# VectorE's 32 by 32 transposes for the decay gates and the root, four row groups of 32 for the gates' products, and another order at the front

## The chip, the cores and the metric

The kernel runs on one core of a Trainium2 chip. The metric is the device time of one execution in microseconds (us). The numbers of the trace come from one profiled execution; its times count from the start of its span.

## What is computed

Two layers (DEPTH = 2) of a mixer on x of 512 tokens by 1024 channels, and a last RMS norm. In each layer (cut to what matters):

```python
h = rmsnorm(x, norm_g)
(qa, ka, va, ga, qb, kb, vb, ab, gb, cq, ckv, kr, gc, mg) = split_cols(h @ w_in)
# branch A: windowed attention; branch C: attention with a low-rank q and kv
# branch B, gated linear attention:
log_a = log_sigmoid(ab @ w_alpha + b_alpha) / B_GATE_TAU        # (512 x 16) @ (16 x 256)
yb = gla_chunk_readout(qb, kb, vb, log_a)
k_rope = apply_rope(kr, cos_c, sin_c)                           # 32 channels, one for all heads of C
m = sigmoid(mg)
y = m[:, :, 0] * za + m[:, :, 1] * zb + m[:, :, 2] * zc
return x + y @ w_out
```

## The kernel before

**Layout.** Channels lie on the partitions and the 512 tokens along the row, in most tensors. A few quantities are wanted the other way round ("natural": 128 tokens on the partitions, in TT = 4 tiles): the keys and values of B, the values of A, the 16 gate inputs ab and the 32 channels kr. They are columns of the four pieces PN1, whose products land in the four banks nat.

**Pieces.** All weights come as 154 pieces of 128 by 1024 (77 per layer), through three buffers raw. ScalarE rounds each piece to w_hi (split_hi, L909), VectorE takes the rest w_lo (split_lo, L1215), and TensorE makes three products for each tile, hi by hi, hi by lo and lo by hi (L657). A piece has four quarters of six products or so. Pieces 0 to 10 are PX (keys of A), PC[0], PC[1], the four PN1, PC[2], PQA[0], PQA[1] and PQB[0].

**Order.** make_schedule writes one list of steps by hand, SCHEDULE, and each engine walks through it in order and does its own part of every step. Nothing is reordered on an engine; between engines semaphores decide. VectorE makes the w_lo of piece p + 2 at quarter 1 of piece p, ScalarE the w_hi of piece p + 3 at quarter 3. Around the change the list is: pieces 0 and 1 with "sum_split" in between (the summed squares of x are split), piece 2, half of piece 3, "rms" (their mean by a product with ones, then logarithm and exponential on ScalarE, one Newton step on VectorE: rstd), "early" (the rope products of the key, two latents), piece 4, **rstd_nat**, lat_sum, piece 5, **rope_k**, piece 6, half of piece 7, **turn_ab**, the other half, **gla_gate**, piece 8, half of piece 9, gla_decay, k_dec.

**The steps that the change touches.**
- rstd_nat: TensorE transposes rstd (L775, four of 128x128) into the bank aux, and VectorE copies one column of each (L1351), so that the root of each token lies on its partition.
- At the end of piece 6 VectorE scales ab and kr by it into k_ab (128 tokens by 4 tiles by 48, L1567) and turns kr by its rope (L1572 to L1576); ScalarE scales A's values (L1006).
- turn_ab: TensorE transposes k_ab (L781, four) into aux, ScalarE copies rows 32 to 47 to ab1, whose row 48 is ones and carries the bias, and rows 0 to 31 to k_rot (L1046, L1048).
- gla_gate: TensorE multiplies ab1 with the weights of the gates, alpha_all, over all 128 rows, most of them zeros in alpha_all (L787, four products, each two instructions). It waits for ab1 and for A's values. The results go to the four banks nat, one each.
- "begin" of a layer: two squares of x are summed, then VectorE makes three small things (L1301 to L1305): the negated sinks, ab1 filled with ones, and zeros ahead of A's values.
- The front: six warm-up products (L744, twelve instructions), the transfers of the first weights (in parts, "heads") and of par_all on ScalarE's queue (L931, L933), then first_pieces (L712 to L722).

Of the kernel before, what the change touches and what calls it, by code (L numbers as in the profile page):

```python
# [19 lines left out]
ALU = mybir.AluOpType  # L20
# [6 lines left out]
TT = S // P  # L27
# [25 lines left out]
WARM = 6  # L53
# [227 lines left out]
AUX = [s for s in SCHEDULE if s[0] in ("rms", "rstd_nat", "gla_end", "latent", "turn_ab")]  # L281
# [23 lines left out]
def build_hybrid_trunk(nc, x_t, pieces, params, alpha, tables, consts, final_g, out, k_rope_dram):  # L305
    with ExitStack() as ctx:
# [76 lines left out]
        k_ab = gates[:, 5, 0:TT * 48].rearrange("p (t n) -> p t n", t=TT)  # L383
        k_prod = gates[:, 5, TT * 48:TT * 112].rearrange("p (i t n) -> p i t n", i=4, t=TT)
# [34 lines left out]
        head_hi, head_lo = sig("head_hi", 0), sig("head_lo", 0)  # L419
# [6 lines left out]
        k_ab_set, k_ab_prod, k_ab_rot, ab_turned = sig("k_ab_set", 4), sig("k_ab_prod", 4), sig("k_ab_rot", 2), sig("ab_turned", 1)  # L426
# [11 lines left out]
        rstd_set = sig("rstd_set", 1)  # L438
        ones_row = sig("ones_row", 1)
# [136 lines left out]
        def _(pe):  # L576
# [121 lines left out]
            def first_pieces():  # L698

                jobs = [(p, k) for p in range(2) for k in range(2)] + [(p, k) for k in range(2, KT) for p in range(2)]  # L700
                for p, k in jobs:
                    if k == 0:
                        pe.wait_ge(proj_free.sem, proj_free.at(0, p - 2))
                        pe.wait_ge(head_hi.sem, p + 1)
                    elif k == 2:
                        pe.wait_ge(head_hi.sem, p + 3)
# [42 lines left out]
            for layer in range(DEPTH):  # L749
                u = 0  # L750
                for name, i in SCHEDULE:
# [150 lines left out]
        def _(act):  # L902
# [49 lines left out]
            head_hi_part(0)  # L952
# [15 lines left out]
            for layer in range(DEPTH):  # L968
                u = 0
                for name, i in SCHEDULE:  # L970
                    if name == "begin":
                        for n in range(1, LATE + 1):
                            square(layer, n)
                    elif name == "split_x" and layer + 1 < DEPTH:
                        split_x(layer + 1, i)
                    elif name == "quarter" and i % 4 == 3:
# [25 lines left out]
                        if p == PN1[3]:  # L1002
                            act.wait_ge(aux_free.sem, aux_free.at(layer, AUX.index(("rstd_nat", 0)) + 1))
                            for t in range(TT):
                                act.wait_ge(k_ab_set.sem, k_ab_set.at(layer, t + 1))
                                nc.scalar.activation(v_a[:, t, :], nat[t][:, 256:384], ACT.Copy,  # L1006
                                                     scale=rstd_nat[:, t:t + 1]).then_inc(v_a_set.sem, 1)
# [21 lines left out]
                        if p == PQB[0]:  # L1029
# [6 lines left out]
                            act.wait_ge(aux_free.sem, aux_free.at(layer, AUX.index(("turn_ab", 0)) + 1))  # L1036
# [145 lines left out]
        def _(dve):  # L1182
# [65 lines left out]
            dve.wait_ge(head_hi.sem, 1)  # L1248
            head_lo_half(*HEADS[0]).then_inc(head_lo.sem, 1)
            for j in range(KT):  # L1250
                split_x(0, j)
                if j in (1, 2):
                    for n in ((1,) if j == 1 else (2, 3)):
                        dve.wait_ge(head_hi.sem, n + 1)
                        head_lo_half(*HEADS[n]).then_inc(head_lo.sem, 1)
                elif j in (3, 4):
                    dve.wait_ge(hi_split.sem, hi_split.at(0, j - 2))
                    head_lo_half(j - 3, slice(512, 1024)).then_inc(lo_split.sem, 1)
            split_lo(0, 2)
            for n in range(LATE + 1, KT + 1):  # L1260
                add_square(-1, n)
            def add_first_rows():
# [30 lines left out]
            for layer in range(DEPTH):  # L1293
                u = 0
                for name, i in SCHEDULE:
                    if name == "split_x" and layer + 1 < DEPTH:
                        split_x(layer + 1, i)
                    elif name == "begin":
                        for n in range(1, LATE + 1):
                            add_square(layer, n)  # L1300
                        nc.vector.tensor_scalar(neg_sink[:, :], par_all[:, layer, SINKS:SINKS + A_HEADS], -1.0, None,  # L1301
# [32 lines left out]
                    elif name == "rope_k":  # L1334

                        dve.wait_ge(proj_free.sem, proj_free.at(layer, by_dve(first_output(PX) + 1)))
                        for g in range(A_KV):
                            rows = slice(32 * g, 32 * g + 32)
                            nc.vector.tensor_tensor(k_a[64 * g:64 * g + 32, :], work[rows, 0, :], work[rows, 1, :],
                                                    ALU.subtract).then_inc(rope_out.sem, 1)  # L1340
                            nc.vector.tensor_tensor(k_a[64 * g + 32:64 * g + 64, :], work[rows, 2, :], work[rows, 3, :],
                                                    ALU.add).then_inc(rope_out.sem, 1)
# [6 lines left out]
                    elif name == "rstd_nat":  # L1349
                        dve.wait_ge(aux_ready.sem, aux_ready.at(layer, u + 1))  # L1350
                        nc.vector.tensor_copy(rstd_nat[:, :], aux[:, :].rearrange("p (t n) -> p t n", t=TT)[:, :, 0]  # L1351
                                              ).then_inc(aux_free.sem, 1)
# [179 lines left out]
                    elif name == "quarter" and i % 4 == 1:  # L1532
                        if (layer, i) != (0, 1) and i // 4 != PUKV:
                            split_lo(layer, i // 4 + 2)
                    elif name == "quarter" and i % 4 == 3:
# [27 lines left out]
                        elif p == PN1[3]:  # L1563
                            evacuated(layer, p)
                            dve.wait_ge(aux_free.sem, aux_free.at(layer, AUX.index(("rstd_nat", 0)) + 1))
# [3 lines left out]
                            dve.wait_ge(k_ab_set.sem, k_ab_set.at(layer, TT))  # L1569
# [202 lines left out]
```

## Time and profile before

| | before |
|---|---|
| median of 3 runs | 932.1 us (931.98 to 932.19) |
| the profiled execution's own time | 931.54 us |
| its span | 929.7 us |
| TensorE products busy | 922.0 us, 99% |
| TensorE weight loads busy | 755.8 us, 81% |
| VectorE busy | 601.2 us, 65% |
| ScalarE busy | 387.2 us, 42% |
| mean granted TensorE clock | 0.999 |

A busy share of a product counts from its start to its modelled end, and products overlap: the full-size ones last 0.39 us and start 0.23 apart. So what an edit on TensorE is worth is read from starts, not from durations. The same holds for VectorE, where a 128x512 instruction lasts 0.69 us and the next one may start 0.60 behind it.

### The profile page before, as it was taken

The numbers are of one execution on the slowest core, as the hardware profiler recorded it, in microseconds if no ns is written. First come the engines' busy times: TensorE is split into PE (matmuls) and PEld (weight loads), VectorE is DVE, ScalarE is ACT, GpSimd is POOL, SyncE is SP. The second block draws the span as 40 slices with busy tenths as digits, with TensorE's granted clock in tenths as the row PEclk, the third lists the DMA queues.
The fourth block names the chain that finished last, engine by engine and source line by source line (L and its number), as shares of the span: only waits on it lengthen the run. The fifth ranks groups of instructions, "written<-read, shape, count | busy, mean of one in ns | idle before, by whom it ended". The sixth has DMA issues, their size and how long they took to land.

```text
span 929.7 us, 13082 instructions
## 1 busy us (share of the span) xinstructions
PE 922.0 (99%) x5108; PEld 755.8 (81%) x5108; DVE 601.2 (65%) x982; ACT 387.2 (42%) x724; POOL 0.2 (0%) x4
## 2 busy tenths in 40 slices
PE   9999999999999999999999999999999999999997
PEld 7988888888888777888889888888888887778886
DVE  7856467448757877575457664674477568876834
ACT  7453344324543454432444333442264425562324
POOL 0000000000000000000000000000000000000000
PEclk9999999999999999999999999999999999999999
DMA  7324324322434255422232333253234433454542
GB/s 292 136 70 147 114 69 136 113 91 80 140 122 140 85 151 150 145 92 90 91 113 91 95 108 106 68 163 109 91 92 143 140 114 109 122 156 136 146 127 90
DMA packets 43789, 110.98 MB, mean 119 GB/s; under 512 B 8592, under 2 KB 11408, under 8 KB 43600
## 3 DMA queue, kind: packets, MB, share of 16 engines
q1 hardware_dynamic: 39664, 104.82, 35.8%
q10 hardware_dynamic: 4064, 5.33, 2.2%
q8 instruction: 40, 0.66, 0.3%
q14 instruction: 21, 0.17, 0.1%
HBM read 85.41 MB, written 2.23 MB: 94 GB/s over the span
## 4 chain that ended last, share of the span: by engine, by line
PE 86%; DVE 5%; ACT 3%; SPq 2%; issue 1%; DMA 1%; ACTq 1%; DVEq 0%
PE ring L657 65%; PE nat L657 9%; PE nat L868 3%; PE aux L892 2%; SPq L495 1%; DVE w_lo L1215 1%; ACT work L1117 1%; PE nat L672 1%; PE nat L671 1%; PE nat L673 1%; DVE work L1514 1%; DMA raw<-pieces 1%; ACT w_hi L909 1%; PE ring L672 1%; PE ring L671 1%
## 5 line engine op out<-in xcount | busy, mean ns | idle before, releaser
L657 PE MATMUL ring<-act_hi,w_hi 128*128 128x512 f32 x784 | 308.7, 394 | 0.0
L657 PE MATMUL ring<-act_lo,w_hi 128*128 128x512 f32 x784 | 305.5, 390 | 0.0
L657 PE MATMUL ring<-act_hi,w_lo 128*128 128x512 f32 x784 | 305.2, 389 | 0.0
L909 ACT ACTIVATE w_hi<-raw 128x1024 fp32r<-128x1024 f32 x152 | 161.7, 1064 | 340.5 <-PE ring L657 275.5
L1215 DVE TENSOR_TENSOR w_lo<-raw,w_hi 128x1024 fp32r<-128x1024 f32 x152 | 184.6, 1216 | 82.7 <-ACT w_hi L909 82.3
L657 PEld LDWEIGHTS ring<-act_hi,w_hi 128*128 128x128 f32 x784 | 147.1, 188 | 38.2 <-issue 8.4
L657 PEld LDWEIGHTS ring<-act_hi,w_lo 128*128 128x128 f32 x784 | 147.2, 188 | 31.1
L657 PEld LDWEIGHTS ring<-act_lo,w_hi 128*128 128x128 f32 x784 | 147.2, 188 | 29.7
L1545 DVE SCALAR_TENSOR_TENSOR gates<-ring,rstd 128x512 f32<-128x512 f32 x72 | 49.3, 685 | 77.0 <-PE ring L657 76.8
L657 PE MATMUL ring<-y_hi,w_hi 128*128 128x512 f32 x192 | 74.9, 390 | 0.0
L657 PE MATMUL ring<-y_hi,w_lo 128*128 128x512 f32 x192 | 74.7, 389 | 0.0
L657 PE MATMUL ring<-y_lo,w_hi 128*128 128x512 f32 x192 | 74.7, 389 | 0.0
L1055 ACT ACTIVATE gates<-gates 128x512 f32<-128x512 f32 x72 | 45.1, 626 | 18.9 <-DVE gates L1545 18.9
L657 PE MATMUL nat<-w_hi,act_hi 128*128 128x512 f32 (+1 forms) x128 | 48.1, 376 | 0.3 <-DVE w_lo L1215 0.3
L657 PE MATMUL nat<-w_lo,act_hi 128*128 128x512 f32 (+1 forms) x128 | 47.8, 374 | 0.0
L657 PE MATMUL nat<-w_hi,act_lo 128*128 128x512 f32 (+1 forms) x128 | 47.8, 374 | 0.0
L1129 ACT ACTIVATE work<-nat,neg_top 128x256 f32<-128x256 f32 (+3 forms) x48 | 24.7, 530 | 43.9 <-DVE neg_top L1472 43.9
L657 PEld LDWEIGHTS ring<-y_hi,w_hi 128*128 128x128 f32 x192 | 36.0, 188 | 8.1 <-issue 0.7
L657 PEld LDWEIGHTS ring<-y_hi,w_lo 128*128 128x128 f32 x192 | 36.0, 188 | 7.5
L657 PEld LDWEIGHTS ring<-y_lo,w_hi 128*128 128x128 f32 x192 | 36.1, 188 | 7.4
L1595 DVE SCALAR_TENSOR_TENSOR gates<-gates,ring 128x512 f32<-128x512 f32 x32 | 21.9, 685 | 9.0 <-PE ring L657 8.9
L657 PEld LDWEIGHTS nat<-w_hi,act_hi 128*128 128x128 f32 x128 | 24.1, 188 | 3.9 <-DVE w_lo L1215 0.8
(227 smaller groups left out, 995.6 us busy)
## 6 DMA issues: line engine op xcount, KB each, us to landing
raw<-pieces SPq DMA_DIRECT2D x152, 512.0 KB, 3.5
bank_g<-work SPq DMA_DIRECT2D x120, 64.0 KB, 2.0
lat<-work SPq DMA_DIRECT2D x72, 64.0 KB, 2.0
bank_g<-work ACTq DMA_DIRECT2D x40, 64.0 KB, 2.2
xt<-x_t SPq DMA_DIRECT2D x8, 256.0 KB, 4.9
bank_a<-work SPq DMA_DIRECT2D x32, 64.0 KB, 2.0
bank_g<-bank_a SPq DMA_DIRECT2D x16, 128.0 KB, 3.9
out<-gates SPq DMA_DIRECT2D x7, 256.0 KB, 2.1
```

What stands on the lines that cost most here:

```text
L495: engine.dma_start(dst[32 * j:32 * j + 32, S * i:S * i + S], work[32 * i:32 * i + 32, 3 + j, :]).then_inc(placed.sem, 16)
L657: mm = pe.matmul(dst, stationary, moving, start=start and i == 0, stop=stop and i == 2)
L671: pe.matmul(bank, act_hi[:, k, ts], w_hi[:, slot, cols], start=k == 0, stop=False)
L672: pe.matmul(bank, act_lo[:, k, ts], w_hi[:, slot, cols], start=False, stop=False)
L868: mm = pe.matmul(nat[a][:, col:col + n], q, k, start=part == 0, stop=part == 2)
L892: mm = pe.matmul(o_t[r * 64:r * 64 + 64, place, :].rearrange("p (i n) -> p i n", i=4), v_c[:, b, h * C_V:(h + 1) * C_V], turned_c[2 - i % ...
L909: nc.scalar.activation(w_hi[:, n % HL, :], raw[:, n % RAW, :], ACT.Copy).then_inc(hi_split.sem, 1)
L1055: nc.scalar.activation(gates[:, j if j >= 4 else 8 + j, :], gates[:, j, :], ACT.Tanh).then_inc(gate_tanh.sem, 1)
L1129: one = nc.scalar.activation(prob[a][:, keys], nat[a][:, keys], ACT.Exp, scale=C_SCALE, bias=neg_top[:, i % 2, 4 * n + a:4 * n + a + 1], a ...
L1215: nc.vector.tensor_tensor(w_lo[:, n % HL, :], raw[:, n % RAW, :], w_hi[:, n % HL, :].bitcast(F32), ALU.subtract).then_inc(lo_split.sem, 1)
L1545: nc.vector.scalar_tensor_tensor(gates[:, j, :], res, 0.5, rstd[:, :], ALU.mult, ALU.mult).then_inc(proj_free.sem, 1)
L1595: nc.vector.scalar_tensor_tensor(merged[:, j, :] if b == 0 else tile, tile, 1.0, z, ALU.add, ALU.mult).then_inc(proj_free.sem, 1)
```

## The change

Four parts:
1. rstd_nat has no product any more. VectorE transposes rstd by itself, in four instructions (one for each group of 32 partitions, 32 by 128), into y_pre, and copies one column of each tile.
2. turn_ab has no product and nothing on ScalarE. k_ab grows to 64 columns a tile, the last 16 filled with ones. VectorE transposes the half with ab in sixteen 32 by 32 blocks into ab1, tile t on the partitions 32t to 32t + 31, and the half with kr in four instructions into k_rot.
3. The gates' four products each use one row group of 32 rows, and alpha_all holds the weights four times.
4. The front: one warm-up product less, par_all sent ahead of the first weights, the first w_hi made by VectorE, the split of piece 3 moved ahead of the last two squares on both engines, and the three small VectorE steps moved from "begin" to rope_k.

```diff
-WARM = 6
+WARM = 5
-AUX = [s for s in SCHEDULE if s[0] in ("rms", "rstd_nat", "gla_end", "latent", "turn_ab")]
+AUX = [s for s in SCHEDULE if s[0] in ("rms", "gla_end", "latent")]
@@ TensorE
-                    elif name == "rstd_nat":
-                        aux_bank(layer, u)
-                        pe.wait_ge(rstd_set.sem, rstd_set.at(layer, 1))
-                        for t in range(TT):
-                            mm = pe.transpose(aux[:, t * P:(t + 1) * P], rstd[:, t * P:(t + 1) * P], ident)
-                    elif name == "turn_ab":
-
-                        aux_bank(layer, u)
-                        pe.wait_ge(k_ab_rot.sem, k_ab_rot.at(layer, 2))
-                        for t in range(TT):
-                            mm = pe.transpose(aux[0:48, t * P:(t + 1) * P], k_ab[:, t, :], ident)
                     elif name == "gla_gate":
 
-                        pe.wait_ge(ab_turned.sem, ab_turned.at(layer, 1))
+                        pe.wait_ge(ab_turned.sem, ab_turned.at(layer, 4 * TT))
                         pe.wait_ge(v_a_set.sem, v_a_set.at(layer, TT))
                         for t in range(TT):
-                            mm = pe.matmul(nat_gate[:, t, :], ab1[:, t * P:(t + 1) * P], alpha_all[:, layer, :],
-                                           start=True, stop=True)
+                            rows = slice(32 * t, 32 * t + 32)
+                            mm = pe.matmul(nat_gate[:, t, :], ab1[rows, 0:P], alpha_all[rows, layer, :], start=True, stop=True)
@@ ScalarE
             for n in range(2):
                 p, cols = HEADS[n]
-                act.dma_start(raw[:, p, cols], pieces[p, :, cols]).then_inc(head_loaded[n].sem, 16)
                 if n == 0:
                     act.dma_start(par_all[:, :, :], params).then_inc(par_loaded.sem, 16)
+                act.dma_start(raw[:, p, cols], pieces[p, :, cols]).then_inc(head_loaded[n].sem, 16)
-            head_hi_part(0)
                     if name == "begin":
+                        if layer == 0:
+                            split_hi(0, RAW)
                         for n in range(1, LATE + 1):
                             square(layer, n)
                         if p + HL < PIECES:
-                            split_hi(layer, p + HL)
+                            if (layer, p) != (0, 0):
+                                split_hi(layer, p + HL)
-                    elif name == "turn_ab":
-                        act.wait_ge(aux_ready.sem, aux_ready.at(layer, u + 1))
-                        act.wait_ge(ones_row.sem, ones_row.at(layer, 1))
-                        nc.scalar.activation(ab1[32:32 + B_RANK, :], aux[32:32 + B_RANK, :],
-                                             ACT.Copy).then_inc(ab_turned.sem, 1)
-                        nc.scalar.activation(k_rot, aux[0:C_ROPE, :], ACT.Copy).then_inc(aux_free.sem, 1)
@@ VectorE
-            dve.wait_ge(head_hi.sem, 1)
-            head_lo_half(*HEADS[0]).then_inc(head_lo.sem, 1)
+            p, cols = HEADS[0]
+            dve.wait_ge(head_loaded[0].sem, 16)
+            nc.vector.tensor_copy(w_hi[:, p, cols], raw[:, p, cols]).then_inc(first_hi.sem, 1)
+            dve.wait_ge(first_hi.sem, 1)
+            head_lo_half(p, cols).then_inc(head_lo.sem, 1)
                     elif name == "begin":
+                        if layer == 0:
+                            split_lo(0, RAW)
                         for n in range(1, LATE + 1):
                             add_square(layer, n)
+                    elif name == "rope_k":
+                        rope_k(layer)
                         nc.vector.tensor_scalar(neg_sink[:, :], par_all[:, layer, SINKS:SINKS + A_HEADS], -1.0, None,
                                                 ALU.mult).then_inc(sink_neg.sem, 1)
                         nc.vector.memset(ab1, 1.0).then_inc(ones_row.sem, 1)
                     elif name == "rstd_nat":
-                        dve.wait_ge(aux_ready.sem, aux_ready.at(layer, u + 1))
-                        nc.vector.tensor_copy(rstd_nat[:, :], aux[:, :].rearrange("p (t n) -> p t n", t=TT)[:, :, 0]
-                                              ).then_inc(aux_free.sem, 1)
+                        turn = y_pre[:, 0:P].rearrange("p (t r) -> p t r", t=TT)
+                        dve.wait_ge(rstd_set.sem, rstd_set.at(layer, 1))
+                        for n in range(4):
+                            rows = slice(32 * n, 32 * n + 32)
+                            nc.vector.transpose(turn[rows], rstd[rows, :].rearrange("p (t n c) -> p t n c", t=TT, n=4)[:, :, n, :]
+                                                ).then_inc(rstd_turned.sem, 1)
+                        dve.wait_ge(rstd_turned.sem, rstd_turned.at(layer, 4))
+                        nc.vector.tensor_copy(rstd_nat[:, :], turn[:, :, 0]).then_inc(rstd_nat_set.sem, 1)
+                    elif name == "turn_ab":
+                        dve.wait_ge(ones_row.sem, ones_row.at(layer, 1))
+                        dve.wait_ge(k_ab_set.sem, k_ab_set.at(layer, TT + 1))
+                        dve.wait_ge(k_ab_rot.sem, k_ab_rot.at(layer, 2))
+                        for t in range(TT):
+                            for n in range(4):
+                                nc.vector.transpose(ab1[32 * t:32 * t + 32, 32 * n:32 * n + 32],
+                                                    k_ab[32 * n:32 * n + 32, t, 32:64]).then_inc(ab_turned.sem, 1)
+                        for n in range(4):
+                            nc.vector.transpose(k_rot.rearrange("p (t n r) -> p t n r", t=TT, n=4)[:, :, n, :],
+                                                k_ab[32 * n:32 * n + 32, :, 0:32]).then_inc(k_turned.sem, 1)
@@ end of piece 6 on VectorE
+                            nc.vector.memset(k_ab[:, :, 48:64], 1.0).then_inc(k_ab_set.sem, 1)
                             for t in range(TT):
-                                nc.vector.tensor_scalar(k_ab[:, t, :], nat[t][:, 384:432], rstd_nat[:, t:t + 1], None,
+                                nc.vector.tensor_scalar(k_ab[:, t, 0:48], nat[t][:, 384:432], rstd_nat[:, t:t + 1], None,
```

## Rows read from the trace of the kernel before

**Rows 1.** The page: busy us of TensorE, share of the span, instructions.

```profile
PE 922.0 (99%) x5108; PEld 755.8 (81%) x5108; DVE 601.2 (65%) x982; ACT 387.2 (42%) x724; POOL 0.2 (0%) x4
```

**Rows 2.** TensorE's waits: line, waited for, us in total, times, longest.

```profile
PE aux L744 <- DVE merged L1232: 1.2, 1, 1.2
PE aux L735 <- DMA bank_g<-work: 0.4, 2, 0.2
PE nat L657 <- DVE w_lo L1215: 0.3, 1, 0.3
```

**Rows 3.** Timeline of TensorE at rstd_nat, layer 0: start, us, engine, line, count.

```profile
33.26 0.60 PE L775 MATMUL aux<-con,rstd 128*128 128x128 f32 x4
...
33.90 0.36 PE L657 MATMUL nat<-w_hi,act_lo 128*128 128x432 f32 x1
34.09 0.36 PE L657 MATMUL nat<-w_lo,act_hi 128*128 128x432 f32 x1
```

**Rows 4.** Timeline of TensorE at gla_gate, layer 1, with the weight load (PEld).

```profile
507.24 1.71 PEld L787 LDWEIGHTS nat<-alpha_all,merged 128*128 128x128 f32 x8
...
507.47 1.89 PE L787 MATMUL nat<-alpha_all,merged 128*128 128x256 f32 x8
...
509.43 0.40 PE L657 MATMUL ring<-act_lo,w_hi 128*128 128x512 f32 x1
```

**Rows 5.** Timeline of TensorE at branch C's scores, second half.

```profile
303.40 1.04 PE L868 MATMUL nat<-bank_g,bank_a 32*128 32x256 f32 x16
...
304.81 0.50 PE L657 MATMUL ring<-y_hi,w_hi 128*128 128x512 f32 x1
305.14 0.39 PE L657 MATMUL ring<-y_lo,w_hi 128*128 128x512 f32 x1
```

**Rows 6.** Timeline of VectorE, layer 1, from rstd_nat to the last latent.

```profile
495.10 0.15 DVE L1351 COPY rstd_nat<-aux 128x4 f32<-128x4 f32 x1
495.17 0.67 DVE L1333 TENSOR_TENSOR merged<-merged 128x512 f32<-128x512 f32 x1
...
499.03 0.68 DVE L1341 TENSOR_TENSOR bank_a<-work 32x512 f32<-32x512 f32 x1
499.75 1.22 DVE L1215 TENSOR_TENSOR w_lo<-raw,w_hi 128x1024 fp32r<-128x1024 f32 x1
501.70 0.79 DVE L1567 TENSOR_SCALAR gates<-nat,rstd_nat 128x48 f32<-128x48 f32 x4 [0.72 <-PE nat L657]
...
503.19 0.22 DVE L1574 TENSOR_TENSOR gates<-gates 128x64 f32<-128x64 f32 x1
...
503.46 1.22 DVE L1215 TENSOR_TENSOR w_lo<-raw,w_hi 128x1024 fp32r<-128x1024 f32 x1
507.67 0.69 DVE L1584 TENSOR_TENSOR gates<-ring,rstd 128x512 f32<-128x512 f32 x1 [2.99 <-PE ring L657]
```

**Rows 7.** Timeline of VectorE at "begin", layer 1.

```profile
471.17 0.17 DVE L1301 TENSOR_SCALAR neg_sink<-par_all 128x8 f32<-128x8 f32 x1
...
471.92 1.16 DVE L1215 TENSOR_TENSOR w_lo<-raw,w_hi 128x1024 fp32r<-128x1024 f32 x1
```

**Rows 8.** Timeline of VectorE at the last of four transposes of gla_norm.

```profile
143.89 0.67 DVE L1412 STREAM_TRANSPOSE work<-bank_a 128x512 f32<-128x512 f32 x1
144.48 1.18 DVE L1215 TENSOR_TENSOR w_lo<-raw,w_hi 128x1024 fp32r<-128x1024 f32 x1
```

**Rows 9.** Timeline of ScalarE at "rms", layer 0.

```profile
24.13 1.28 ACT L1061 ACT_TABLE_LOAD   x1
26.41 0.69 ACT L914 ACTIVATE merged<-aux,eps 128x512 f32<-128x512 f32 x1 [0.99 <-PE aux L770]
```

**Rows 10.** Timeline at gla_decay, layer 1: VectorE's log_a and TensorE's products.

```profile
513.62 1.22 DVE L1360 SCALAR_TENSOR_TENSOR gates<-nat,gates 128x1024 f32<-128x1024 f32 x1 [2.41 <-ACT gates L1070]
...
517.41 1.89 PE L794 MATMUL nat<-gates,con 128*128 128x256 f32 x8
```

**Rows 11.** One line's instructions, L744: ns min/median/max, first and last start, forms.

```profile
L744 PE MATMUL aux<-merged x12: 380/634/796, 1.2 to 5.9; 128*128 128x256 f32 x12
```

More of the change, by code:

```diff
@@ L382, in build_hybrid_trunk @@
         latent = gates[:, 2:5, :]
-        k_ab = gates[:, 5, 0:TT * 48].rearrange("p (t n) -> p t n", t=TT)
-        k_prod = gates[:, 5, TT * 48:TT * 112].rearrange("p (i t n) -> p i t n", i=4, t=TT)
+        k_ab = gates[:, 5, 0:TT * 64].rearrange("p (t n) -> p t n", t=TT)
+        k_prod = gates[:, 5, TT * 64:TT * 128].rearrange("p (i t n) -> p i t n", i=4, t=TT)
         k_cos, k_sin = [con[:, K_TABLE + 64 * i:K_TABLE + 64 * i + 64].rearrange("p (t n) -> p t n", t=TT) for i in range(2)]
@@ L418, in build_hybrid_trunk @@
         head_loaded = [sig(f"head_loaded{n}", 0) for n in range(4)]
-        head_hi, head_lo = sig("head_hi", 0), sig("head_lo", 0)
+        first_hi, head_hi, head_lo = sig("first_hi", 0), sig("head_hi", 0), sig("head_lo", 0)
         eps_set, ones_set = sig("eps_set", 0), sig("ones_set", 0)
@@ L425, in build_hybrid_trunk @@
         ring_act = sig("ring_act", by_act(first_output(PIECES)))
-        k_ab_set, k_ab_prod, k_ab_rot, ab_turned = sig("k_ab_set", 4), sig("k_ab_prod", 4), sig("k_ab_rot", 2), sig("ab_turned", 1)
+        k_ab_set, k_ab_prod, k_ab_rot, ab_turned = sig("k_ab_set", TT + 1), sig("k_ab_prod", 4), sig("k_ab_rot", 2), sig("ab_turned", 4 * TT)
         q_placed = sig("q_placed", 256)
@@ L438, in build_hybrid_trunk @@
         rstd_set = sig("rstd_set", 1)
+        rstd_turned, rstd_nat_set, k_turned = sig("rstd_turned", TT), sig("rstd_nat_set", 1), sig("k_turned", 4)
         ones_row = sig("ones_row", 1)
@@ L703, in first_pieces @@
                         pe.wait_ge(proj_free.sem, proj_free.at(0, p - 2))
-                        pe.wait_ge(head_hi.sem, p + 1)
+                        pe.wait_ge((first_hi, head_hi)[p].sem, 1)
                     elif k == 2:
-                        pe.wait_ge(head_hi.sem, p + 3)
+                        pe.wait_ge(head_hi.sem, p + 2)
                     elif k == KT // 2:
@@ L1002, in _ @@
                         if p == PN1[3]:
-                            act.wait_ge(aux_free.sem, aux_free.at(layer, AUX.index(("rstd_nat", 0)) + 1))
+                            act.wait_ge(rstd_nat_set.sem, rstd_nat_set.at(layer, 1))
                             for t in range(TT):
-                                act.wait_ge(k_ab_set.sem, k_ab_set.at(layer, t + 1))
+                                act.wait_ge(k_ab_set.sem, k_ab_set.at(layer, t + 2))
                                 nc.scalar.activation(v_a[:, t, :], nat[t][:, 256:384], ACT.Copy,
@@ L1034, in _ @@
                             act.dma_start(v_as[64:128, :, :], v_a[0:64, :, :]).then_inc(v_shifted.sem, 16)
-                            act.wait_ge(aux_free.sem, aux_free.at(layer, AUX.index(("turn_ab", 0)) + 1))
+                            act.wait_ge(k_turned.sem, k_turned.at(layer, 4))
                             act.dma_start(k_rope_dram, k_rot).then_inc(k_rope_saved.sem, 16)
@@ L1253, in _ @@
                     for n in ((1,) if j == 1 else (2, 3)):
-                        dve.wait_ge(head_hi.sem, n + 1)
+                        dve.wait_ge(head_hi.sem, n)
                         head_lo_half(*HEADS[n]).then_inc(head_lo.sem, 1)
@@ L1261, in _, with rope_k @@
                 add_square(-1, n)
+            def rope_k(layer):
+                dve.wait_ge(proj_free.sem, proj_free.at(layer, by_dve(first_output(PX) + 1)))
+                for g in range(A_KV):
+                    rows = slice(32 * g, 32 * g + 32)
+                    nc.vector.tensor_tensor(k_a[64 * g:64 * g + 32, :], work[rows, 0, :], work[rows, 1, :],
+                                            ALU.subtract).then_inc(rope_out.sem, 1)
+                    nc.vector.tensor_tensor(k_a[64 * g + 32:64 * g + 64, :], work[rows, 2, :], work[rows, 3, :],
+                                            ALU.add).then_inc(rope_out.sem, 1)
             def add_first_rows():
@@ L1333, in _ @@
                         nc.vector.tensor_tensor(sq_sum, sq[0], sq[1], ALU.add).then_inc(lat_acc.sem, 1)
[L1334 to L1342, printed above, removed]
                     elif name == "k_dec":
@@ L1532, in _ @@
                     elif name == "quarter" and i % 4 == 1:
-                        if (layer, i) != (0, 1) and i // 4 != PUKV:
+                        if (layer, i) not in ((0, 1), (0, 5)) and i // 4 != PUKV:
                             split_lo(layer, i // 4 + 2)
@@ L1564, in _ @@
                             evacuated(layer, p)
-                            dve.wait_ge(aux_free.sem, aux_free.at(layer, AUX.index(("rstd_nat", 0)) + 1))
+                            dve.wait_ge(rstd_nat_set.sem, rstd_nat_set.at(layer, 1))
+                            nc.vector.memset(k_ab[:, :, 48:64], 1.0).then_inc(k_ab_set.sem, 1)
                             for t in range(TT):
-                                nc.vector.tensor_scalar(k_ab[:, t, :], nat[t][:, 384:432], rstd_nat[:, t:t + 1], None,
+                                nc.vector.tensor_scalar(k_ab[:, t, 0:48], nat[t][:, 384:432], rstd_nat[:, t:t + 1], None,
                                                         ALU.mult).then_inc(k_ab_set.sem, 1)
-                            dve.wait_ge(k_ab_set.sem, k_ab_set.at(layer, TT))
+                            dve.wait_ge(k_ab_set.sem, k_ab_set.at(layer, TT + 1))
                             k1, k2 = k_ab[:, :, 0:16], k_ab[:, :, 16:32]
@@ L1751 @@
     rows = np.zeros((P, DEPTH, B_HEADS * B_DK), x.dtype)
-    rows[32:32 + B_RANK] = w_alpha.transpose(1, 0, 2)
-    rows[32 + B_RANK] = b_alpha
+    for t in range(TT):
+        rows[32 * t:32 * t + B_RANK] = w_alpha.transpose(1, 0, 2)
+        rows[32 * t + B_RANK] = b_alpha
     arrays = {
```

## The prediction

> **What bounds the kernel now.** I read the page first, then TensorE's waits, then its order of time around the three steps that the diff touches, and last VectorE's. TensorE is busy for 922.0 of 929.7 us, and all the waits that TensorE's view lists sum to 1.9 us, 1.2 of them before its first warm-up product [rows 1, 2]. So the kernel is a queue of products in a fixed order: each product taken out is worth its step on TensorE, as long as nothing that TensorE waits for becomes late by more than its slack. The question is therefore what the change does to VectorE just ahead of the decay gates' products (gla_gate, L787), where their input ab1 comes from.
>
> **What TensorE loses in work.** A step is the distance of two starts. The four transposes of rstd_nat start at 33.26, the second piece product behind them at 33.90, one more at 34.09 [rows 3]. Without them the products would start at 33.26 and 33.46, so they cost 33.90 - 33.46 = 0.44 us. The four of turn_ab are as long and stand in the same pattern, in both layers, so I take the same price. Both together: 0.88 us per layer.
> The gates' eight products start at 507.47, and the second product behind them at 509.43; their first weight load was at 507.24 [rows 4]. In four row groups the nearest rows are the scores of branch C, 32 rows by 256 columns, four neighbours in four groups and four banks, as the new gates would be: 24 instructions (the 16 of the row and 8 left out) between 303.40 and 304.81, 59 ns each, then 0.33 us to the second product behind [rows 5]. Eight of them are 0.47 us, and from the first load to the second product behind them 0.47 + 0.33 = 0.80 us, where it was 509.43 - 507.24 = 2.19. That is 1.39 us less if the input is there. If the groups did not overlap, this would be about 0.1.
>
> **What VectorE gets.** In layer 1 it runs without a pause from the root's refinement to the w_lo of piece 8, and it has just 0.72 us of idle time, at 501.70, before the work of the gates begins [rows 6]. Along this chain I add:
> (a) rstd_nat: one copy with a step of 0.07 (495.10 to 495.17) becomes four transposes of 32 by 128 and a copy.
> (b) The step rope_k takes in three small ones from "begin" (the negated sinks and two memsets): 471.17 to 471.92, 0.75 us [rows 7].
> (c) A memset of 64 elements, 0.10 (an estimate: a little over the 0.07 step of the copy of 4 elements).
> (d) turn_ab: sixteen transposes of 32 by 32, then four of 32 by 128.
> No row has such a small transpose. A transpose of 128x512 lasts 0.67 us and a step of 0.59 follows it [rows 8]; TENSOR_TENSOR of 64 columns lasts 0.22 and of 512 0.69, so 1.05 ns a column. From this a 32-column transpose lasts 0.67 - 480 x 1.05 ns = 0.17 us and a 128-column one 0.26. What matters is whether the next may start before the last has ended. In most rows it may: of the two 64-wide ones that start at 503.19 each lasts 0.22, yet the w_lo behind both starts 0.27 later. In the rope of k it may not: each instruction works on another group of 32 partitions than the last, there is no wait between them, and the one at 499.03 lasts 0.68 and the next starts 0.72 behind it (all four steps there are 0.71 or 0.72) [rows 6]. The new transposes change their group at every instruction, as those do. So I take the nearest row: duration plus 0.035, that is 0.20 for each of the sixteen and 0.30 for the wide ones; the ends are 0.10 (overlapped) and 0.24 (if filling the transposer adds as long again as 32 columns, 0.034).
> The Trainium skill, page "VectorE: DVE Perf Modes", section "Two Vector instructions with no wait between them", states this as a rule: an instruction whose input or output begins in another quadrant than before starts only when all earlier ones have finished. The rope rows agree. The same page's section "The three transpose paths" lists VectorE's transpose as quicker than TensorE's, which alone would speak for the overlapped price and the first rival's time.
>
> The chain in layer 1, in starts: (a) three held steps of 0.30 + 0.26 to the copy + 0.03 = 1.20, then 0.07, so lat_sum starts at 496.37 instead of 495.17: 1.20 later. With (b) the w_lo of piece 8 starts at 499.75 + 1.95 = 501.70. It takes a step of 1.13, so the gates' input is scaled from 502.83; before, this waited for TensorE until 501.70. The memset 0.10, the work up to the next w_lo 503.46 - 501.70 = 1.76, that w_lo (piece 9) 1.13: the sixteen transposes start at 505.82. Fifteen held steps of 0.20 and one duration of 0.17: ab1 is ready at 508.99, for TensorE at 509.02. TensorE would have been there at 507.24 - 0.88 = 506.36. It waits **2.7 us**, and its second product behind the gates starts at 509.02 + 0.80 = 509.82 instead of 509.43: 0.39 us lost, though 2.3 us of its work are gone.
> Layer 0 has the same distances (copy 36.70, w_lo 45.08, same steps). It has the front too. The parameters' transfer ahead of the first weights, the first w_hi on VectorE, and one warm-up product less (two of the 12 instructions of L744) may let the first real product start up to 0.4 us earlier. The split of piece 3, put ahead of two squares, removes the wait of 0.3 us for w_lo [rows 2]. But both end at the same gate wait: TensorE only gets there earlier, while VectorE's chain starts with the logarithm at 26.41. That had 0.99 us of slack behind the table load, 24.13 + 1.28 = 25.41 [rows 9]. The moved split (1.05 us on ScalarE) puts the summed squares and so the table load 1.05 us later, to 26.46, and the logarithm at about 26.48, 0.07 late. So the front brings nothing, or costs 0.1.
> Moved VectorE work (b) frees "begin", where only that same sum waited for it. The four wide transposes for k behind ab1 last 4 x 0.30 = 1.2 us; behind them queue the latent's scaling (507.67 before, now about 510.3), ScalarE's three latent steps, and the gates' soft plus, all back to back. So log_a ends about 2.3 us later than at 514.84, at 517.2, and TensorE's decay products come at 517.41 + 0.39 = 517.8 (load about 0.2 before) [rows 6, 10]. They are just covered, with 0.4 us; the w_lo of pieces 6 to 11 have over 1 us each except that of piece 6, which lies ahead of (a) and does not move.
> **Sum:** 2 x 0.39 + 0.07 = +0.85 us. The profiled execution took 931.54 us (span 929.7) against a median of 932.1, so I put the difference on the median: **933.0 us**, 0.1% more, within the 0.2% (1.9 us) that a measurement can tell from no change.
>
> **Rivals.**
> 1. The small transposes overlap, as the 64-wide rows do: 0.10 and 0.20 a step. Then (a) costs 0.89, the sixteen 15 x 0.10 + 0.17 = 1.67, ab1 is ready at 507.21 and the second product behind starts at 508.01: 1.4 us won per layer, 2.8 in all, 929.3. The diff asks for no wait between them, which speaks for it; the rope rows speak against it. Chance 0.20.
> 2. Slower: each small transpose pays the filling of its 32 columns apart, 0.034 us more for each of twenty per layer. That is 0.68 per layer, 934.4. It decides from 0.024 us more per transpose (0.95 us over 40). For it: no row shows a transpose so short. Against it: the 128x512 one lasts no longer than a TENSOR_TENSOR. Chance 0.20.
> 3. TensorE's clock falls in the wait. It stands still for 2.7 us in layer 1 and about 3.4 in layer 0, where nothing before stood over 0.4. At the start the products of L744 last 0.63 us and only the last ones 0.38, after about 4 us of work [rows 11]; 4 us at half the clock is 2 us of work lost: 935.0 if in one layer, 937 in both. The page "TensorE: Matmul & The Clock Gate" of the Trainium skill, section "Why this matters for your kernels", asks for no idle gaps of this order between bursts. Chance 0.07.
> 4. The change does not do what it says: the gates' products don't run side by side. Then each layer loses 1.27 more, 935.5. The scores' rows speak against it. Chance 0.03.
> The forecast itself has 0.50, with an own range of 932.0 to 933.9 (0.02 us per transpose either way).
>
> **Numbers.** Faster by over 0.2% is below 930.2: rival 1 and a little for waits that I count too long, 0.21. Slower is above 934.0: rivals 2 to 4, 0.30. Within: 0.49. The range takes in rivals 1 and 2 and one fallen clock: 929.2 to 935.1.
>
> **What would show it.** In the new trace: a wait of TensorE at the gates' products for VectorE's transposes, 2.7 us in layer 1 and about 3.4 in layer 0; starts of the sixteen 0.20 apart; the gates' eight products within 0.5 us; no wait at the decay products; the wait of 0.3 us on w_lo gone. The prediction is wrong if those starts are 0.10 apart, or if TensorE waits elsewhere (the decay products first, whose slack is 0.4), or if ab1 is ready before 507.6 in layer 1's times of before, from where the change wins over 0.2%.

## The result and the profile after

| | before | after |
|---|---|---|
| median | 932.05 us (4 runs) | 937.26 us (4 runs, 937.06 to 938.64) |
| ratio, after to before | | 1.0062, 95% interval 1.0049 to 1.0074 |
| the profiled execution | 931.54 us | 937.12 us |
| its span | 929.7 us | 935.3 us |
| mean granted TensorE clock | 0.999 | 0.995 |

The change made the kernel 0.6% slower, 5.2 us. The forecast was 933.0 with a range of 929.2 to 935.1: the sign of the difference was right, its size was wrong, and the time lies outside the range. In the page, TensorE is busy for 1.0 us less than in [rows 1], though the span is 5.6 us longer:

```profile
span 935.3 us, 13088 instructions
...
PE 921.0 (98%) x5090; PEld 753.5 (81%) x5090; DVE 612.4 (65%) x1033; ACT 384.7 (41%) x719; POOL 0.2 (0%) x4
```

TensorE's waits (waited for: us in total, times, longest) answer to [rows 2]. The wait at piece 3 is gone, and a new one at the gates' products holds 6.5 us in two times:

```profile
PE nat L778 <- DVE merged L1358: 6.5, 2, 3.6
PE aux L745 <- DVE merged L1218: 1.2, 1, 1.2
PE aux L736 <- DMA bank_g<-work: 0.4, 2, 0.2
```

VectorE's order of time in layer 1, from rstd_nat to the last latent, answers to [rows 6]. It is one chain without a pause, as forecast:

```profile
497.97 1.30 DVE L1348 STREAM_TRANSPOSE y_pre<-rstd 32x128 f32<-32x128 f32 x4
499.31 0.17 DVE L1351 COPY rstd_nat<-y_pre 128x4 f32<-128x4 f32 x1
499.38 0.69 DVE L1336 TENSOR_TENSOR merged<-merged 128x512 f32<-128x512 f32 x1
...
503.97 0.17 DVE L1304 TENSOR_SCALAR neg_sink<-par_all 128x8 f32<-128x8 f32 x1
...
504.73 1.15 DVE L1201 TENSOR_TENSOR w_lo<-raw,w_hi 128x1024 fp32r<-128x1024 f32 x1
505.84 0.11 DVE L1576 MEMSET gates<- 128x64 f32 x1
505.88 0.71 DVE L1578 TENSOR_SCALAR gates<-nat,rstd_nat 128x48 f32<-128x48 f32 x4
...
507.58 1.22 DVE L1201 TENSOR_TENSOR w_lo<-raw,w_hi 128x1024 fp32r<-128x1024 f32 x1
508.71 3.71 DVE L1358 STREAM_TRANSPOSE merged<-gates 32x32 f32<-32x32 f32 x16
512.45 1.30 DVE L1361 STREAM_TRANSPOSE merged<-gates 32x128 f32<-32x128 f32 x4
```

And TensorE's order of time there, which answers to [rows 4]. After a standstill of 2.90 us come the gates' products, a first full-size product at the usual distance behind such a group (0.34; it is 0.33 in gate_later below), a second one that is followed after 0.39 instead of 0.23, and then products that last 0.63 us and start 0.43 apart:

```profile
509.19 0.39 PE L658 MATMUL ring<-act_hi,w_lo 128*128 128x512 f32 x1
512.48 0.71 PE L778 MATMUL nat<-alpha_all,merged 32*128 32x256 f32 x8 [2.90 <-DVE merged L1358]
513.12 0.50 PE L658 MATMUL ring<-act_hi,w_hi 128*128 128x512 f32 x1
513.46 0.59 PE L658 MATMUL ring<-act_lo,w_hi 128*128 128x512 f32 x1
513.85 0.63 PE L658 MATMUL ring<-act_hi,w_lo 128*128 128x512 f32 x1
514.27 0.63 PE L658 MATMUL ring<-act_hi,w_hi 128*128 128x512 f32 x1
...
516.83 0.43 PE L658 MATMUL ring<-act_hi,w_hi 128*128 128x512 f32 x1
```

That is the clock at its lower level, 1.2 GHz. In a table by stretches (from and to, length, busy time and count of PE, of PEld, of DVE, of ACT and of POOL, granted clock, DMA share, GB/s) it stands at 0.50 behind both gate waits; this is layer 1:

```profile
512.00:513.00 1.00, 0.52 (x8) 0.31 (x8) 0.91 (x4) 0.00 (x0) 0.00 (x0) 1.00 0.00 0
513.00:514.00 1.00, 1.00 (x7) 0.74 (x4) 0.91 (x4) 0.00 (x0) 0.00 (x0) 0.74 0.00 0
514.00:515.00 1.00, 1.00 (x4) 0.81 (x3) 0.47 (x1) 0.50 (x1) 0.00 (x0) 0.50 0.00 0
515.00:516.00 1.00, 1.00 (x4) 0.71 (x4) 0.69 (x1) 0.97 (x3) 0.00 (x0) 0.50 0.00 0
516.00:517.00 1.00, 1.00 (x4) 0.81 (x3) 0.65 (x1) 1.00 (x2) 0.00 (x0) 0.55 0.00 0
517.00:518.00 1.00, 1.00 (x6) 0.81 (x5) 0.04 (x1) 0.97 (x2) 0.00 (x0) 1.00 0.00 0
```

**Where the 5.6 us of the span come from.** The second product behind the gates is the mark that the prediction used. In layer 0 it starts at 52.28 instead of 51.05, so 1.23 us are lost there. Layer 1's rstd_nat comes at 497.97 instead of 495.10, 2.87 late, so 2.87 - 1.23 = 1.64 us were lost between, and the disturbance that stands in that stretch is the clock. (Product by product: when TensorE's steps are 0.23 again, at 56.38, it is 2.79 late, so 1.56 of the 1.64 lie in the slow products themselves, and 0.08 elsewhere.) In layer 1 the mark comes at 513.46 instead of 509.43, 4.03 late, so 1.16 lost at the gates. The span ends 5.60 late, 1.57 more. Together: 2.39 us at the gates, 3.21 us by the clock. This is the pair of profiled executions; the medians differ by 5.2 us.

### The profile page after: what moved, and what is told of

It reads as the page before. It is cut to its first block, busy times and chain, and to the rows that moved or that the text cites. A ratio compares the mean times of both kernels' runs of the same rounds, so it can differ in the third digit from the quotient of the medians.

```text
span 935.3 us, 13088 instructions
## 1 busy us (share of the span) xinstructions
PE 921.0 (98%) x5090; PEld 753.5 (81%) x5090; DVE 612.4 (65%) x1033; ACT 384.7 (41%) x719; POOL 0.2 (0%) x4
## 4 chain that ended last, share of the span: by engine, by line
PE 82%; DVE 9%; ACT 4%; issue 2%; SPq 1%; DMA 1%; ACTq 1%; DVEq 0%
PE ring L658 64%; PE nat L658 5%; PE nat L858 3%; PE aux L882 2%; DVE w_lo L1201 2%; SPq L496 1%; ACT work L1103 1%; ACT w_hi L899 1%; PE nat L674 1%; PE nat L672 1%; PE nat L673 1%; DVE work L1524 1%; DVE merged L1358 1%; PE ring L674 1%; PE ring L672 1%
## 5 line engine op out<-in xcount | busy, mean ns | idle before, releaser
L1524 DVE STREAM_TRANSPOSE work<-work 128x512 f32<-128x512 f32 x42 | 26.9, 683 | 0.0
```

Source lines behind the costliest of these rows:

```text
L1524: nc.vector.transpose(blocks[:, :, k, :, :].rearrange("p j h r -> p h j r"), prob[k].rearrange("p (h j c) -> p h j c", h=GROUP, j=4)).then ...
```

## The experiments

Two questions: what the transposes' price is made of, and whether the clock's fall follows from the standstill. Then, whether the chain ahead of the gates is all that spoils the change. The last experiments answer this by shortening the chain. The kernel before ran beside all of them, with a median of 931.8 us.

**fill_wait: products in the wait.**

```diff
                     elif name == "gla_gate":
+                        pe.wait_ge(aux_free.sem, aux_free.at(layer, 1))
+                        for _ in range(10):
+                            pe.matmul(aux[:, :], act_hi[:, 0, 0:P], act_hi[:, 0, :], start=True, stop=True)
                         pe.wait_ge(ab_turned.sem, ab_turned.at(layer, 4 * TT))
```

> The changed kernel with ten full-size products more on TensorE (0.23 us each, into the bank aux, results unused) in front of the wait for the gates' input, so that TensorE stands still for about 1.3 us in layer 0 and 0.6 us in layer 1, not 3.6 and 2.9. Theory: the fallen clock costs 1.6 us per layer, and it falls because of the standstill. Then the products behind the gates stay 0.23 us apart and the time is 937.3 - 3.2 = 934.1 us. Rival: the clock falls for another reason (the 32-row products themselves), then it stays at 937.3.

Measured: 934.01 us (933.69 to 934.88). TensorE's first wait in its list:

```profile
PE nat L781 <- DVE merged L1361: 1.9, 2, 1.3
```

The granted clock is 1.00 in every stretch around both gates, and the products behind the gates start at 52.14 and 52.47, and from there on 0.23 apart. The kernel does more work and is 3.25 us faster. So the fallen clock costs the 3.2 us that the two traces had shown, and it falls because TensorE stands still. The rival is excluded: the 32-row products were there as before.

**same_group: all small transposes on the same 32 partitions.**

```diff
-                                nc.vector.transpose(ab1[32 * t:32 * t + 32, 32 * n:32 * n + 32],
-                                                    k_ab[32 * n:32 * n + 32, t, 32:64])
+                                nc.vector.transpose(ab1[0:32, P * t + 32 * n:P * t + 32 * n + 32],
+                                                    k_ab[0:32, t, 32:64])
```

> The changed kernel with all sixteen small transposes reading and writing partitions 0 to 31 (their blocks beside each other along the row), so the gates' input is wrong and the output is not the reference's. Theory: a transpose that begins in another group of 32 partitions than the last waits for its end; inside one group the starts come closer, to 0.10 to 0.14 us from 0.23. The input is ready 1.5 to 2.0 us earlier per layer, and the clock may stay up: 931 to 934 us. Rival: filling the transposer sets the distance, whatever the group: 0.23 us as before and 937.3 us.

This kernel leaves out the spreading of the blocks over the groups, so its output is not the reference's; only its times are used. Measured: 929.86 us (929.64 to 931.69), ratio 0.9982 (0.9973 to 0.9992). VectorE at turn_ab in layer 0, and the line's durations (ns, least, median and most):

```profile
47.76 1.59 DVE L1358 STREAM_TRANSPOSE merged<-gates 32x32 f32<-32x32 f32 x16
...
L1358 DVE STREAM_TRANSPOSE merged<-gates x32: 156/156/193, 47.8 to 506.6; 32x32 f32<-32x32 f32 x32
```

Inside one group the sixteen take 1.59 us, so they start (1.59 - 0.16) / 15 = 0.095 apart and last 0.156. In the changed kernel they take 3.71:

```profile
L1358 DVE STREAM_TRANSPOSE merged<-gates x32: 193/202/207, 47.5 to 512.2; 32x32 f32<-32x32 f32 x32
```

They start (3.71 - 0.20) / 15 = 0.234 apart there and last 0.202. The held start is shown; the change of the group costs 0.14 us per transpose, 2.1 us per layer. The edit moves input and output to one group at once, so it doesn't tell which of the two matters. TensorE's waits shrank to 1.48 and 0.77 us, and the clock stayed at 1.00. It came out 1.1 us below the lower end of what I expected. The two prices add up to it: 2.1 us in each layer and the 3.2 us of the clock make 7.4, and 937.26 - 7.4 = 929.9.

**ab_first: turn_ab ahead of the w_lo of piece 9.**

```diff
     piece(PN1[3])
-    half(PC[2], 0)
     step(("turn_ab", 0))
+    half(PC[2], 0)
     half(PC[2], 1)
```

> The changed kernel with turn_ab ahead of the w_lo of piece 9 on VectorE. The input is ready 1.13 us earlier, so TensorE waits about 2.5 us in layer 0 and 1.8 in layer 1. If the clock stays up at that, 937.3 - 2.3 - 3.2 = 931.8 us; if it still falls in both layers, 935.0 us; in one, 933.4.

Measured: 934.39 us (934.13 to 935.42). The profiled execution is the slowest of the six, 935.42 us, and shows the outcome with the clock fallen in both layers. The input came 0.91 us earlier per layer, not 1.13: behind the last rope step, on whose result they wait, the transposes start after 0.35 us (506.64 and 506.99 in layer 1), where in the change the w_lo starts after 0.14. That gives 937.26 - 2 x 0.91 = 935.4, as this execution took. The other five took 934.1 to 934.6, about 1.0 less; whether the clock fell less in them can't be told without a trace of one. The standstills were 2.65 and 1.98 us, and behind both the clock is at 0.50 (the second shown; columns: stretch, length, busy share and count of PE, granted clock, DMA share, GB/s):

```profile
511.00:512.00 1.00, 1.00 (x11) 1.00 0.00 0
512.00:513.00 1.00, 1.00 (x5) 0.71 0.00 0
513.00:514.00 1.00, 1.00 (x4) 0.50 0.00 0
```

**split_back: piece 3 split where it was before** (the lines of the diff with split_hi(0, RAW) and split_lo(0, RAW) undone).

> The changed kernel with the split of piece 3 where it was before. Theory: in layer 0 TensorE only waits 0.5 us less at the gates, since the chain of VectorE sets their time and starts 0.1 us earlier: 937.1 to 937.3 us, unless the clock then stays up in layer 0 (a standstill of about 3.1 us; at 2.0 and 2.7 it fell). Rival: the split is worth its 0.5 us also here, 937.8.

Measured: 936.85 us (936.72 to 937.87), ratio 1.0057 (1.0043 to 1.0071) beside the change's 1.0062 (1.0049 to 1.0074), so by the times no difference that can be told. TensorE's waits at the gates are 5.8 us in all instead of 6.5, 2.88 in each layer, and the clock fell in both.

The trace shows more. The wait at piece 3 is gone here too: with the three small steps out of "begin", the w_lo of piece 3 starts at 21.64 instead of 22.08 before, and TensorE loses only about 0.2 us at piece 3. And the moved split is not free for VectorE's chain. ScalarE's logarithm, where that chain starts, comes 0.46 us earlier without it (this run, then the change):

```profile
26.04 0.69 ACT L904 ACTIVATE merged<-aux,eps 128x512 f32<-128x512 f32 x1 [0.59 <-PE aux L771]
26.50 0.69 ACT L904 ACTIVATE merged<-aux,eps 128x512 f32<-128x512 f32 x1
```

So in layer 0 the gates' input is ready 0.46 us earlier too: their products start at 50.84 instead of 51.30. The split's gain is absorbed by the gate wait, and its price of 0.46 us is paid there. The medians lie 0.4 us apart in that sense, which agrees but is too little to prove it.

In layer 0 of this execution the clock was down before work had begun again, and the gates' eight products already ran slowly: 1.16 us to the next one, not 0.64 (TensorE, then the stretches with the columns of ab_first's):

```profile
50.84 1.23 PE L778 MATMUL nat<-alpha_all,merged 32*128 32x256 f32 x8 [2.88 <-DVE merged L1353]
52.00 0.80 PE L658 MATMUL ring<-act_hi,w_hi 128*128 128x512 f32 x1
52.60 0.63 PE L658 MATMUL ring<-act_lo,w_hi 128*128 128x512 f32 x1
```

```profile
50.00:51.00 1.00, 0.16 (x4) 0.57 0.06 25
51.00:52.00 1.00, 1.00 (x8) 0.50 0.06 16
```

This fall cost 2.8 us: from the gates' start at 50.84 the fourteenth full-size product is reached at 57.38, 6.54 us later, where the steps at the upper level (0.98 to the second product, then twelve of 0.23) would make 3.74. The one in layer 1, behind a standstill of the same 2.88 us, cost 1.6. So the price of a fall is not the same each time. The profiled execution took 937.87 us, 1.0 over the median, which fits.

**front_only: the front alone, on the kernel before.**

> The kernel before with the front alone changed (one warm-up product less, the parameters' transfer first, the first w_hi on VectorE, the split of piece 3 ahead of two squares); transposes, gates and memsets as before. Theory: the start gives nothing (the first act_lo comes no earlier), the split removes the wait of 0.3 us at piece 3, 0.5 us with the cold first product behind it, and since nothing here waits for the longer chain of the root, it stays: 931.3 us. Rival: that gain is lost at rstd_nat or turn_ab, then 931.8 as before.

Measured: 931.17 us (930.84 to 931.53), ratio 0.9994 (0.9984 to 1.0003). The size is as expected, though the interval does not exclude no change. The trace shows where it comes from, TensorE at the start:

```profile
5.80 0.47 PE L712 MATMUL ring<-act_hi,w_hi 128*128 128x512 f32 x1
6.21 0.51 PE L719 MATMUL ring<-act_hi,w_lo 128*128 128x512 f32 x1
6.88 0.51 PE L722 MATMUL ring<-act_lo,w_hi 128*128 128x512 f32 x1 [0.16 <-DVE act_lo L1243]
...
22.66 0.39 PE L657 MATMUL ring<-act_hi,w_lo 128*128 128x512 f32 x1
22.88 0.35 PE L657 MATMUL nat<-w_hi,act_hi 128*128 128x432 f32 x1
```

The first product starts 0.28 earlier than before (6.08), but the third, which needs act_lo, starts at 6.88 instead of 6.78. The start brings nothing; the wait at piece 3 is gone, and the product there starts at 22.88 instead of 23.29.

**late_rope: the chain ahead of the gates shortened by all that can wait.** On top of ab_first:

```diff
     piece(PN1[2])
-    step(("rope_k", 0))
     piece(PN1[3])
...
-    step(("gla_decay", 0), ("gla_end", 0), ("k_dec", 0))
+    step(("rope_k", 0), ("gla_decay", 0), ("gla_end", 0), ("k_dec", 0))
...
-                        nc.vector.memset(ab1, 1.0).then_inc(ones_row.sem, 1)
...
-                        dve.wait_ge(ones_row.sem, ones_row.at(layer, 1))
...
+                            else:
+                                dve.wait_ge(rope_out.sem, rope_out.at(layer, 4))
```

> As ab_first, and rope_k with two of its small steps moved behind the w_lo of piece 11, ahead of gla_decay, where VectorE has 2.4 to 3.1 us of idle time; the memset of the gates' input, now without use, left out. Theory: only VectorE's chain ahead of the gates spoils the change. The sixteen transposes then begin 1.7 us behind the last product of piece 6, TensorE waits under 0.5 us, the clock stays up, and the work taken from TensorE shows: 2.1 us per layer and 0.6 at the front, so 927.5 to 928.5 us. Rival: a wait moves to the decay products or to a bank of the ring, 930 us or more.

Measured: 929.24 us (928.97 to 929.97), ratio 0.9974 (0.9964 to 0.9983). TensorE's waits:

```profile
PE nat L777 <- DVE merged L1355: 0.6, 2, 0.3
PE nat L783 <- DVE gates L1367: 0.5, 2, 0.3
```

That is 0.7 us above the range I had given, 927.5 to 928.5. Both theories were partly right. The gates wait only 0.3 us a layer and the kernel is faster than before. But the second line is the rival's: the decay products now wait for log_a.

**k_later: the last latent ahead of the w_lo of piece 9 and of the transposes for k.** On top of late_rope:

```diff
     half(PC[2], 1)
+    step(("turn_k", 0))
     step(("gla_gate", 0))
...
+                    elif name == "turn_k":
                         for n in range(4):
                             nc.vector.transpose(k_rot.rearrange("p (t n r) -> p t n r", t=TT, n=4)[:, :, n, :],
...
-                        if (layer, i) not in ((0, 1), (0, 5)) and i // 4 != PUKV:
+                        if (layer, i) not in ((0, 1), (0, 5)) and i // 4 not in (PUKV, PC[2]):
...
                             nc.vector.tensor_tensor(latent[:, 2, :], res, rstd[:, :],
                                                     ALU.mult).then_inc(proj_free.sem, 1)
+                            split_lo(layer, p + 2)
```

> As late_rope (rope_k moved, turn_ab ahead of the w_lo of piece 9), and on VectorE the scaling of the last latent comes first behind the sixteen transposes, then the w_lo of piece 9, then the four transposes for k. In late_rope the decay products waited 0.3 us per layer for log_a, which hangs on that latent through ScalarE. It now comes about 2.3 us earlier. Theory: this wait goes, 0.3 to 0.5 us per layer: 929.2 - 0.8 = 928.4 us. Rival: the lost time of late_rope against its forecast lies elsewhere, 929.2.

Measured: 928.14 us (927.85 to 928.16), ratio 0.996 (0.9948 to 0.9973). The wait at the decay products is gone from TensorE's list; that at the gates is unchanged (0.6 in two times).

**gate_later: the gates' products six products later.** On top of k_later:

```diff
-    step(("gla_gate", 0))
-    piece(PQA[0])
+    step(("quarter", 4 * PQA[0]), ("gla_gate", 0), *(("quarter", 4 * PQA[0] + q) for q in range(1, 4)))
```

> As k_later, with the gates' products one quarter (six products, 1.4 us) later on TensorE. The last wait there, 0.3 us per layer with a cold weight load behind it, should go, and log_a hangs on ScalarE's latent steps, not on the products, so nothing else comes later: 928.4 - 0.7 = 927.7 us. Rival: log_a is late then and the decay products wait, 928.4 or more.

Measured: 927.23 us (927.14 to 927.47), ratio 0.9952 (0.9939 to 0.9964). No wait at the gates or at the decay products is left. TensorE at the gates, layer 1, and VectorE ahead of them, layer 0:

```profile
505.30 0.39 PE L657 MATMUL ring<-act_hi,w_lo 128*128 128x512 f32 x1
505.62 0.71 PE L777 MATMUL nat<-alpha_all,merged 32*128 32x256 f32 x8
506.27 0.50 PE L657 MATMUL ring<-act_hi,w_hi 128*128 128x512 f32 x1
506.60 0.40 PE L657 MATMUL ring<-act_lo,w_hi 128*128 128x512 f32 x1
```

```profile
44.30 3.72 DVE L1355 STREAM_TRANSPOSE merged<-gates 32x32 f32<-32x32 f32 x16
48.05 0.69 DVE L1595 TENSOR_TENSOR gates<-ring,rstd 128x512 f32<-128x512 f32 x1
48.65 1.22 DVE L1200 TENSOR_TENSOR w_lo<-raw,w_hi 128x1024 fp32r<-128x1024 f32 x1
49.79 1.29 DVE L1359 STREAM_TRANSPOSE merged<-gates 32x128 f32<-32x128 f32 x4
```

The transposes are as slow as in the change, 3.72 us for sixteen. They only stand where nothing waits for them. This kernel has all of the change's edits on TensorE, though the gates' products stand six products later, and beats both: 4.6 us faster than before, 10.0 than the change.

## Why the prediction was wrong

- **What bounds the kernel, and where the change would be decided: right.** The chain, the wait at the gates, which nothing covers, and the missing wait at piece 3 are all in the trace. Standstills: forecast 2.7 and about 3.4 us, listed by the trace as 2.90 and 3.58. These are not counted alike: the prediction counts from where the gates' first load would stand, beside the start of the last full-size product, the trace from that product's end. By the prediction's count they were 3.3 and 4.0 (509.19 to 512.48 and 47.33 to 51.30), 0.6 us more than forecast.
- **Held transposes: right in kind** (same_group), **short in size.** I had a held transpose last 0.17 us with a step of 0.20; it lasts 0.202 with a step of 0.234. Sixteen took 3.71 us instead of 3.17. The duration had been worked out along TENSOR_TENSOR's slope from rows that were not held. A transpose that is not held does last 0.156, near the 0.17; a held one lasts 0.046 longer, which no row of before had shown for a short one. The wide ones also last longer than I had put them, 0.30 instead of 0.26, so that (a) cost 1.34 instead of 1.20. Rival 2's sum (0.034 more for each of twenty) fits the starts, but whether filling the transposer is the cause was not tried.
- **The gates' products: one term too small.** Eight instructions took 0.64 us (512.48 to 513.12), not 0.47. I had scaled 24 neighbours in 1.41 us down to eight, as if a group had no fixed part; through the two groups, 24 in 1.41 and eight in 0.64, goes an estimate of 0.048 us each and 0.26 for the group. To the second product behind it was 0.98, not 0.80. The same 0.65 stands in gate_later (505.62 to 506.27), where nothing is waited for. Rival 4 is out: start to start the group takes 0.64 us, where it was 1.53 (507.47 to 509.00), and products one behind the other would have made the loss larger by 1.27, not by 0.18.
- **(b) and (c):** 0.76 us for 0.75, and 0.04 for 0.10.
- **The sum at the gates:** layer 1 lost 1.16 instead of 0.39. The misses are +0.54 (sixteen), +0.14 (wide ones), +0.18 (gates), -0.12 (memset and the work behind it), rest 0.03. Layer 0 has the same, 1.23 instead of 0.46.
- **The clock: the step that failed.** I had 2.7 and 3.4 us of standstill in the sum and the cost of a fall about right (2 us for each; measured 1.64 and 1.57 here, and 2.8 in one layer of split_back), but put the fall at nothing in the sum and gave it 0.07, as an alternative to the forecast. It was a consequence of it: the two falls make 3.2 of the 5.6 us, and the gates 2.4 where I had 0.85. It fell in all six standstills between 1.98 and 3.58 us that the change, ab_first and split_back show, and in none of the four up to 1.48 us in fill_wait and same_group. Rivals 2 and 3 both came true in part, on top of the forecast; I had treated them as excluding each other, so the range ended at 935.1 where their sum, 0.85 + 1.4 + 4 above 932.1, would have been 938.4.
- **The front: right for the change as a whole, wrong in its parts.** The logarithm came 0.09 us later than before (26.50, 26.41), forecast 0.07, and front_only shows that the earlier start gains nothing by itself. But split_back shows that the three steps out of "begin" had by themselves ended the wait at piece 3, and that without the moved split the logarithm would have come at 26.04. The split cost the chain 0.46 us in the changed kernel, which I did not see.
- **The slack of 0.4 us at the decay products: right.** The change did not touch it, since TensorE came late itself. It was the next limit as soon as TensorE was early (late_rope, 0.3 us), as the prediction's last paragraph named it.
- **What I passed over:** I took the order of VectorE's work as given. 2.9 us of rope_k and 1.1 us of w_lo stood ahead of the transposes and could wait, and a memset there (0.48 us) had no use any more.

## What to carry to other kernels

Work that is moved from the full engine to a half-idle one is free only at its place: read the receiving engine's chain up to the next thing the full engine waits for, and first move out of that chain whatever is not needed there. The same edits cost 5.2 us in one order and won 4.6 in a better one. A forecast wait on TensorE of a length at which the clock has been seen to fall (here 1.98 us and more) is to be priced twice, once for its length and once for the clock behind it. And many small VectorE instructions that step from one group of 32 partitions to the next are to be costed at their full held distance, here 0.234 us and not 0.095.

## What the runs showed of the hardware

- With a standstill of 1.98 to 3.58 us TensorE's granted clock fell from 2.4 to 1.2 GHz, six times of six, at a cost of about 1.6 us in five of them and 2.8 us in one (split_back, layer 0); with 0.63 to 1.48 us, four times of four, it did not fall. The moment differs from one to the next. In layer 1 of the change the gates' products and the first full-size one still ran at full speed before the products came 0.43 us apart; in ab_first's layer 1 four full-size ones did; in split_back's layer 0 the clock was already at 0.50 when the gates' products began. Ten idle products in the wait kept it up (fill_wait, 3.25 us won). The Trainium skill, page "TensorE: Matmul & The Clock Gate", section "Why this matters for your kernels", advises against idle gaps between bursts of products; the rows at 0.50 behind the standstills agree. The gap from which it warns is longer than the 1.98 us with which the clock fell here; the measurement decides.
- A 32 by 32 transpose of float32 on VectorE lasts 0.156 us and the next starts 0.095 behind it on the same 32 partitions; with its input in another group each time (and its output in another every fourth time) it lasts 0.202 and the next starts 0.234 behind. That the held ones also last longer I had not expected. The Trainium skill's rule of held instructions (page "VectorE: DVE Perf Modes", section "Two Vector instructions with no wait between them") agrees with the starts and says nothing of the durations.
- Eight 32 by 256 products in four row groups take 0.64 us from their start to the next full-size one, where a share of a longer run (24 in 1.41 us) had given 0.47.
